# Where the squares of a norm are summed, and when two weight tiles are split: two gated MLPs in a hybrid decoder trunk

## The reference, cut to what matters

```python
def rmsnorm(x, g):
    xf = f32(x)
    return xf * lax.rsqrt(jnp.mean(xf * xf, axis=-1, keepdims=True) + RMS_EPS) * f32(g)

def conv_ffn(x, g, w_up, conv_w, conv_b, w_down):      # D_FF = 2816, CONV_WIDTH = 3
    u = f32(rmsnorm(x, g).astype(x.dtype) @ w_up)
    up = jnp.pad(u, ((0, 0), (CONV_WIDTH - 1, 0), (0, 0)))
    c = f32(conv_b) + sum(f32(conv_w[j]) * up[:, j:j + T] for j in range(CONV_WIDTH))
    gate, val = jnp.split(c, 2, axis=-1)
    return (jax.nn.silu(gate) * val).astype(x.dtype) @ w_down
```

## Time and profile before

| | |
|---|---|
| device time, median of 3 runs | 1308.78 us (1308.62 to 1309.12) |
| the profiled execution's own time | 1308.9 us |
| span of its instructions | 1307.0 us |
| TensorE matmuls busy | 1275.2 us, 98% of the span |
| VectorE / ScalarE / GpSimd busy | 76% / 49% / 25% |
| granted TensorE clock, mean | 1.00 |

### The profile page before, as it was taken

The page is one execution under the profiler, slowest core; times in us unless marked ns, Lnnn a source line. Parts: engine busy times, 40 slices in busy tenths (PEclk is TensorE's granted clock), DMA queues, the critical chain, the costliest instruction groups (busy, mean ns, idle before and its releaser), DMA issues.

```text
span 1307.0 us, 27113 instructions
## 1 busy us (share of the span) xinstructions
PE 1275.2 (98%) x10688; PEld 1041.3 (80%) x10688; DVE 992.2 (76%) x1486; ACT 646.0 (49%) x1068; POOL 321.3 (25%) x302
## 2 busy tenths in 40 slices
PE   7999999999999999999999999999999999999999
PEld 5876777776578888988889988776778889888898
DVE  4777777787468889857889958548578899578896
ACT  6575645563244445334546555547554453344542
POOL 3369777784420000000001256330100000000000
PEclk9999999999999999999999999999999999999999
DMA  8100111114023332233332342211133323333331
GB/s 326 49 22 32 55 55 40 55 32 168 18 97 97 96 108 90 86 104 96 96 105 90 112 143 81 65 49 33 33 98 97 96 89 122 97 96 98 119 109 46
DMA packets 30055, 114.35 MB, mean 87 GB/s; under 512 B 3456, under 2 KB 5248, under 8 KB 29184
## 3 DMA queue, kind: packets, MB, share of 16 engines
q1 hardware_dynamic: 29952, 112.89, 26.0%
HBM read 110.78 MB, written 2.10 MB: 86 GB/s over the span
## 4 chain that ended last, share of the span: by engine, by line
PE 86%; DVE 5%; ACT 3%; issue 1%; POOL 0%; DVEq 0%; POOLq 0%; ACTq 0%
PE bank L665 84%; PE bank L1384 1%; DVE arena L2132 1%; ACT arena L1581 1%; PE bank L971 0%; DVE sin_part L2696 0%; DVE cos_part L2723 0%; DVE in_lo L2143 0%; PE bank L1266 0%; DVE head_stat L2706 0%; ACT w_hi L1464 0%; DVE w_lo L2118 0%; PE bank L1289 0%; DVE stat L2210 0%; DVE cos_part L2692 0%
## 5 line engine op out<-in xcount | busy, mean ns | idle before, releaser
L665 PE MATMUL bank<-in_hi,w_hi 128*128 128x512 f32 x704 | 274.9, 390 | 0.9 <-DVE in_lo L2143 0.9
L665 PE MATMUL bank<-in_lo,w_hi 128*128 128x512 f32 x704 | 273.9, 389 | 0.0
L665 PE MATMUL bank<-in_hi,w_lo 128*128 128x512 f32 x704 | 273.9, 389 | 0.0
L1464 ACT ACTIVATE w_hi<-ring 128x1024 fp32r<-128x1024 f32 (+2 forms) x176 | 161.4, 919 | 205.2 <-PE bank L665 204.9
L665 PE MATMUL bank<-z,w_hi 128*128 128x256 f32 (+1 forms) x1088 | 221.9, 303 | 0.7 <-DVE w_lo L2118 0.7
L665 PEld LDWEIGHTS bank<-z,w_hi 128*128 128x128 f32 x1088 | 175.9, 191 | 9.7 <-DVE w_lo L2118 0.9
L2118 DVE TENSOR_TENSOR w_lo<-ring,w_hi 128x1024 fp32r<-128x1024 f32 (+2 forms) x156 | 161.1, 1035 | 26.4 <-ACT w_hi L1464 25.0
L665 PE MATMUL bank<-z,w_lo 128*128 128x256 f32 (+1 forms) x544 | 164.1, 302 | 0.0
L665 PEld LDWEIGHTS bank<-in_hi,w_hi 128*128 128x128 f32 x704 | 132.2, 188 | 29.6 <-DVE in_lo L2143 1.3
L665 PEld LDWEIGHTS bank<-in_lo,w_hi 128*128 128x128 f32 x704 | 132.2, 188 | 27.7 <-issue 0.5
L665 PEld LDWEIGHTS bank<-in_hi,w_lo 128*128 128x128 f32 x704 | 132.1, 188 | 27.4
(11 more groups left out here) (292 smaller groups left out, 2239.3 us busy)
## 6 DMA issues: line engine op xcount, KB each, us to landing
ring<-w_ring SPq DMA_DIRECT2D x119, 512.0 KB, 3.5
ring<-w_ring SPq DMA_DIRECT2D x32, 704.0 KB, 4.1
ring<-w_pairs SPq DMA_DIRECT2D x18, 512.0 KB, 3.9
arena<-w_mem SPq DMA_DIRECT2D x2, 2048.0 KB, 19.0
arena<-w_ring SPq DMA_DIRECT2D x4, 512.0 KB, 4.9
x<-xT SPq DMA_DIRECT2D x1, 2048.0 KB, 8.5
outT<-x SPq DMA_DIRECT2D x8, 256.0 KB, 2.0
mask<-masks SPq DMA_DIRECT2D x1, 1536.0 KB, 7.0
```

The costliest lines, as they stand in the source:

```text
L665: return nc.tensor.matmul(out, lhsT, rhs, start=first, stop=last, skip_group_check=True)
L1464: return nc.scalar.activation(out, in_, ACT.Copy)
```

## The change

1. The squares are summed whole: also slice 7 is added into `y[:, 0, :]`, and `square_sum` is one product by ones, of `y[:, 0, :]`, in place of two.
2. That product moves from between up 0 and up 1 into up 1: ahead of slice 2 of it in the first MLP, ahead of slice 7 (the last) in the second.
3. The first MLP's seven adds are GpSimd's. The second MLP's seven adds leave GpSimd, and stand on VectorE's list between `residual` and the MLP.
4. In pair 0 of an MLP's first half, the split of up 3 is put right behind the root on ScalarE and behind the reciprocal on VectorE, ahead of both reads and own taps.
5. The counts that are waited for are rewritten with `squares_summed` for the new numbers of adds (7, 6, 7; the middle sum, of the stream between the layers, stays at 6 adds).

```diff
+        def squares_summed(q, n):
+            return (0, KD - 1, 2 * KD - 3)[q] + n
...
             def square_sum(q):
-                pe.wait_ge(sem("sq_sum"), (KD - 2) * (q + 1))
-                mm(bank[7][:, :], ones, y[:, 0, :], True, False)
-                pe.wait_ge(sem("xsq"), KD * (q + 2))
-                mm(bank[7][:, :], ones, y[:, KD - 1, :], False, True).then_inc(sem("x_ss"), 1)
+                pe.wait_ge(sem("sq_sum"), squares_summed(q, KD - 1))
+                mm(bank[7][:, :], ones, y[:, 0, :]).then_inc(sem("x_ss"), 1)
...
                         for s in range(2):
-                            if half == 0 and q == 0 and s == 1:
-                                square_sum(2 * l)
+                            sum_at = (2, KD - 1)[l] if half == 0 and q == 0 and s == 1 else None
...
                             split_product(bank[b][:, :], n, in_hi, in_lo, KD,
+                                          between=lambda k: square_sum(2 * l) if k == sum_at else None,
...
+                        elif half == 0 and q == 0:                       # ScalarE
+                            split_at(p, up + 2, q)
+                            stream_root(2 * l + 1)
+                            split_at(p, up + 3, q)
+                            own_tap(0)
+                            own_tap(1)
+                            gate()
                         else:
                             for s in range(2):
                                 split_at(p, up + 2 + s, q)
-                                if half == 0 and q == 0 and s == 0:
-                                    stream_root(2 * l + 1)
                                 own_tap(s)
                             gate()
...
+                        if half == 0 and q == 0:                         # VectorE
+                            split(up + 2)
+                            stream_rstd(2 * l + 1)
+                            split(up + 3)
                         for s in range(2):
-                            if half == 0 and q == 0 and s == 0:
-                                split(up + 2)
-                                stream_rstd(2 * l + 1)
                             read(s)
-                            if half or q or s:
+                            if half or q:
                                 split(2 * p + (up + 2 + s), up + 2 + s + 2 * q)
...
             residual(N_OUTB, 3, 0.5)                                     # VectorE
+            for m in range(1, KD):
+                dve.wait_ge(sem("xsq"), 3 * KD + m + 1)
+                if m > 1:
+                    dve.wait_ge(sem("sq_sum"), squares_summed(2, m - 1))
+                V.tensor_tensor(y[:, 0, :], y[:, 0, :], y[:, m, :], ALU.add).then_inc(sem("sq_sum"), 1)
             mlp(1, 0)
...
-            sum_squares(0)                                               # GpSimd
-            sum_squares(1)
+            sum_squares(0, KD - 1)
+            sum_squares(1, KD - 2)
...
-            sum_squares(2)
```

More of the change, by code:

```diff
@@ L1247, in token_sums @@
             def token_sums():
-                pe.wait_ge(sem("sq_sum"), 2 * (KD - 2))
+                pe.wait_ge(sem("sq_sum"), squares_summed(1, KD - 2))
                 pe.wait_ge(sem("xsq"), 3 * KD)
@@ L1920, in _ @@
             mlp(0)
-            act.wait_ge(sem("sq_sum"), 2 * (KD - 2))
+            act.wait_ge(sem("sq_sum"), squares_summed(1, KD - 2))
             def group_done(g, r):
@@ L3006, in _, with sum_squares @@
                 G.tensor_tensor(out_low[k], y[:, k, :], out_high[k].bitcast(F32), ALU.subtract).then_inc(sem("y_split"), 1)
-            def sum_squares(q):
-                for m in range(1, KD - 1):
+            def sum_squares(q, last):
+                for m in range(1, last + 1):
                     pool.wait_ge(sem("xsq"), KD * (q + 1) + m + 1)
                     if m > 1:
-                        pool.wait_ge(sem("sq_sum"), (KD - 2) * q + m - 1)
+                        pool.wait_ge(sem("sq_sum"), squares_summed(q, m - 1))
                     G.tensor_tensor(y[:, 0, :], y[:, 0, :], y[:, m, :], ALU.add).then_inc(sem("sq_sum"), 1)
-            sum_squares(0)
-            sum_squares(1)
+            sum_squares(0, KD - 1)
+            sum_squares(1, KD - 2)
             pool.wait_ge(sem("w_lo"), N_PROJ + 2 - N_SPLIT)
```

## The result

| | median | runs | lowest to highest |
|---|---|---|---|
| before | 1308.97 us | 5 | 1308.62 to 1309.28 |
| changed | 1315.38 us | 5 | 1314.97 to 1315.89 |

The ratio is 1.0047, with a 95% interval of 1.0036 to 1.0058: slower by 6.4 us. The forecast was slower, at 1312.1 us, with a range up to 1314.4; the measured time lies 1.0 us above the range and 3.3 us above the forecast. The profiled execution took 1315.89 us, with a span of 1314.1 us; before it was 1308.9 and 1307.0.

A forecast was written before the change was run, and what follows sets the result against it. TensorE, busy 1275.2 of 1307.0 us, was taken as the bound. Up 4 starting 1.24 us later in the first MLP and 2.08 in the second added 3.3 us, giving 1312.1 us from the median 1308.78; range 1309.6 to 1314.4.

The forecast's parts named there:

- A rule that speaks further against it: Second MLP's stall: a long gap without matmuls drops the clock to 1.2 GHz, 1.7 us more; kept out of the sum.
- the second wait: Second MLP, before up 4: TensorE waits 4.2 us for the low half, so up 4 effectively starts 2.08 us later.
- the first wait, of 2.0 us: First MLP, before up 4: TensorE stalls for the low half, so up 4 effectively starts 1.24 us later.
- the sum: Both MLPs' delays of up 4 added, 1.24 + 2.08 = 3.3 us, with no price for a clock fall.
- The row that the prediction set against a fall: Short gap before 953.36: after 1.3 us without a matmul none is slow, so nothing extra, 1312.1.
- read 0 at 398.75 forecast: First MLP, VectorE: read 0 starts 2.77 us later than its former 395.98, behind the split of up 3.
- The seventh add of GpSimd: First MLP: it slows VectorE's low half of up 1, ending by 389.4, needed at 389.95; costed at nothing.
- forecast 0.73, bounds 0.69 and 0.9: Second MLP's seven adds on VectorE: 5.1 us in all, no wait; at 0.9 a step, a wait of 0.6 us.
- TensorE's entry by 1.46 us: Second MLP, start of up 0: without GpSimd's adds slowing VectorE, TensorE no longer waits for in_lo and gains 1.46 us.
- The rival that the stretch from read 0 shortens: VectorE, read 0 to split of up 4: moving up 3's split out shortens each stall 1.1 us, 1309.9; chance 0.16.
- The rival that the lateness is absorbed: Before up 4 in both MLPs: no new stall, so TensorE keeps 3.2 us of savings, 1305.6; chance 0.10.

The follow-up runs named there:

- e3: The changed kernel plus unused filler matmuls on TensorE between up 1 and up 2, 8 in the first MLP and 17 in the second: 1312.41 us, ratio 1.0024.
- e2: The kernel before with only the new order of the splits, keeping two products and six adds on GpSimd: 1314.82 us, ratio 1.0038.
- e6: The kernel before with the second MLP's six adds on VectorE instead of GpSimd, four inside the residual's waits, two behind it: 1308.35 us, ratio 0.9994.
- e4: The changed kernel with the old split order, earlier products and four of the second MLP's adds in VectorE's residual gaps: 1306.05 us, ratio 0.9975.
- e1: The changed kernel with the old order of the splits, the split of up 3 between the two reads: 1310.70 us, ratio 1.0009.
- e7: The version with adds in the gaps and early products, but with the new order of the splits: 1311.95 us, ratio 1.0021.

## Why the prediction was right and wrong

**Wrong: the clock.** The step that failed is the one headed "A rule that speaks further against it". It put the fall of the clock into the range only, and for the second wait only; the first wait, of 2.0 us, got no price for the clock at all, and the sum had none. Measured: a fall behind both waits in the profiled execution, 1.6 us each (1.7 was the price taken from the kernel's start), and a clock of 0.997 in all five timed executions, 1315.0 to 1315.9 us, where one fall would give some 1313.7. 3.3 + 2 x 1.6 = 6.5, against 6.4 measured. e3 takes the idle time away without taking work away and comes out at 1312.4, by 0.3 the forecast's own number.

The row that the prediction set against a fall does not bear the weight. Its 1.3 us before 953.36 run from the start of one matmul to the start of the next; the idle time there is 0.90 us, as the bracket says. Counted from start to start the first new wait is 2.3 us (407.33 to 409.65), in idle time 1.93. The longest idle time of the kernel before, behind its start, is 1.66 us, between other matmuls (64 by 64), and the clock stays at 1.00 there:

```profile
106.91 1.10 PE L665 MATMUL bank<-arena 64*64 64x128 f32 x32 [1.66 <-DVE arena L2185]
```

Nor do the matmuls right behind a wait settle the matter: the clock can fall a while after TensorE has restarted, 1.6 us in the changed kernel (411.21) and 0.6 us in e2 (410.67). The rule of the Trainium skill (TensorE: Matmul & The Clock Gate, HAM oscillation), that a long enough gap without matmuls drops the clock, is borne out in kind. How short a wait has to be to be free of it was not tried.

**Right: the first MLP.** Wait 2.0 forecast, 2.1 measured in the same count; start of up 4 later by 1.13 forecast (the 1.24 takes in 0.11 for the restart), 1.28 measured; read 0 at 398.75 forecast, 398.90 without the start's shift. The seventh add of GpSimd made the split of up 1 take 2.31 us, and it ended in time, as forecast.

**Right: the second MLP.** Up 0 without a wait, adds of 0.78 us a step (forecast 0.73, bounds 0.69 and 0.9) hidden by up 1, product on time, wait of 4.2 forecast, 4.25 measured in the same count; start of up 4 later by 1.97 forecast (2.08 less the restart), 1.94 measured. That GpSimd's adds had slowed VectorE, and with it TensorE's entry by 1.46 us, is shown by the trace after, where no wait is left, and by e6.

**Right: which part does the harm.** The rival that the stretch from read 0 shortens is refuted (10.36 us against 10.35). The rival that the lateness is absorbed is refuted in this kernel, but its 1305.6 is nearly what e4 reaches (1306.05) by getting the sum early instead of late and leaving the order alone. In the first MLP the order alone makes the wait: it is gone in e1, where the product keeps its new place. In the second both parts do. The wait there is 4.09 us with the late sum and the new order, 2.88 with the late sum alone (e1), 1.93 with the new order alone (e2, e7), and none with neither (e4). Going back to the old order returns 4.7 of the 6.4 us (e1).

Not settled: why the clock fell behind the first wait of 1.93 us in the profile of e2 and not behind the second, equally long one. Executions of the same kernel differ in it: 3 of 5 of e2 and 9 of 11 of e7 show a fall with two such waits each, and 9 of 11 of e1 with one wait of 2.88 us. So a kernel with such a wait has a time that depends on it.

## What to carry to other kernels

When a split or copy is moved ahead of a read, look at what it waits for itself: here its slot became free only when the tile before last was off TensorE, so the read, with the chain behind it, was tied to an engine that it hadn't waited for. A wait of TensorE is to be priced with what may follow it, the matmuls at the lower clock level, which here doubled the loss; a filler in a test shows the share. Removing work from a full engine pays only if the other engines still meet its next deadline: the 0.9 us saved twice on TensorE brought nothing, since VectorE came 2.8 us later to a deadline that it had met with 1.7 and 0.9 us to spare.

## What the runs showed that was not expected

- Behind idle times of 1.93 us the slow matmuls began 1.6 us behind the restart in the changed kernel, 0.6 us behind it in e2, and not at all behind the second wait of e2 and both of e7 in their profiles; behind 2.88 and 4.09 us they began at once.
- The record of the granted clock notes both falls (0.50), but 1.00 at the kernel's start, where the matmuls behind the first have the same distance of 0.43 us.
- Seven dependent adds of 0.69 us on VectorE took 5.46 us, 0.78 a step, 0.09 more than each alone.
